# A language model's two blocks on one core: all sixteen tiles of the second mixer turned by token behind the attention units

## What is computed

```
def step(S, inp):
    r_t, w_t, k_t, v_t, a_t, b_t = inp
    Sa = jnp.einsum('bhij,bhj->bhi', S, a_t)
    S = S * w_t[:, :, None, :] + Sa[..., None] * b_t[:, :, None, :] + v_t[..., None] * k_t[:, :, None, :]
    return S, jnp.einsum('bhij,bhj->bhi', S, r_t)
...
o_fox = forgetting_attention(fh(fq), fh(fk), fh(fv), ff, fox_forget_bias[l])
o_rwkv = rwkv7_time_mix(p_rwkv, shift_mu[l], ...)
mix = jnp.concatenate([o_fox, o_rwkv], axis=-1) @ w_out[l]
```

## Time and profile before

| | us |
|---|---|
| median of 3 runs | 3400.59 |
| lowest, highest | 3396.19, 3407.8 |
| the profiled execution | 3394.34 |
| its span | 3392.6 |

### The profile page before, as it was taken

The page is one execution under the profiler, slowest core; times in us unless marked ns, Lnnn a source line. Parts: engine busy times, 40 slices in busy tenths (PEclk is TensorE's granted clock), DMA queues, the critical chain, the costliest instruction groups (busy, mean ns, idle before and its releaser), DMA issues.

```text
span 3392.6 us, 50022 instructions
## 1 busy us (share of the span) xinstructions
PE 3306.0 (97%) x18459; PEld 2704.5 (80%) x18459; DVE 1931.4 (57%) x3749; ACT 1254.7 (37%) x1622; POOL 132.2 (4%) x54
## 2 busy tenths in 40 slices
PE   8998999999899999999999999999999999999998
PEld 6665877878577788888878887888888888888886
DVE  5455456552565544452355999998885444444443
ACT  3333233322455433342343334444544333333332
POOL 0000000000000000000001545000000000000000
PEclk9987999999999999999999999999999999999999
DMA  4110012323222222222332444455556655555542
GB/s 145 56 38 1 4 51 81 99 93 100 86 65 67 80 76 79 80 74 93 100 106 79 148 141 143 156 180 182 185 177 220 228 198 192 198 194 196 198 142 81
DMA packets 145995, 408.03 MB, mean 120 GB/s; under 512 B 11225, under 2 KB 43993, under 8 KB 143585
## 3 DMA queue, kind: packets, MB, share of 16 engines
q1 hardware_dynamic: 73520, 265.85, 25.7%
q10 hardware_dynamic: 72368, 140.68, 11.5%
HBM read 337.28 MB, written 69.21 MB: 120 GB/s over the span
## 4 chain that ended last, share of the span: by engine, by line
PE 87%; DVE 10%; ACT 1%; issue 1%; DMA 1%; ACTq 0%; DVEq 0%; SPq 0%
PE bank L337 24%; PE bank L339 24%; PE bank L338 24%; PE bank L959 2%; PE bank L445 2%; PE bank L957 2%; PE bank L889 1%; ACT arena L1000 1%; PE bank L464 1%; DVE arena L2057 1%; PE bank L503 1%; DVE arena L2020 1%; DVE arena L2021 1%; DVE arena L2023 1%; PE bank L372 1%
## 5 line engine op out<-in xcount | busy, mean ns | idle before, releaser
L337 PE MATMUL bank<-xs,ring_hi 128*128 128x512 f32 x2488 | 990.9, 398 | 19.9 <-DVE xs L1564 9.7
L339 PE MATMUL bank<-xs,ring_lo 128*128 128x512 f32 x2488 | 971.8, 391 | 0.0
L338 PE MATMUL bank<-xs,ring_hi 128*128 128x512 f32 x2488 | 971.3, 390 | 0.0
L1000 ACT ACTIVATE arena<-bank 128x512 f32<-128x512 f32 (+4 forms) x584 | 392.1, 706 | 1013.1 <-PE bank L339 726.8
L1000 ACT ACTIVATE ring_hi<-ring 128x1024 fp32r<-128x1024 f32 x503 | 532.4, 1061 | 621.4 <-DMA ring<-weights 425.3
L1557 DVE TENSOR_TENSOR ring_lo<-ring,ring_hi 128x1024 fp32r<-128x1024 f32 x246 | 300.2, 1224 | 519.5 <-ACT ring_hi L1000 484.0
L337 PEld LDWEIGHTS bank<-xs,ring_hi 128*128 128x128 f32 x2488 | 468.8, 188 | 127.9 <-issue 14.4
L339 PEld LDWEIGHTS bank<-xs,ring_lo 128*128 128x128 f32 x2488 | 468.3, 188 | 100.9
L338 PEld LDWEIGHTS bank<-xs,ring_hi 128*128 128x128 f32 x2488 | 469.2, 189 | 97.1 <-issue 3.4
L2070 DVE TENSOR_TENSOR ring_lo<-ring,ring_hi 128x1024 fp32r<-128x1024 f32 x206 | 252.6, 1226 | 387.3 <-ACT ring_hi L1000 387.2
L337 PE MATMUL bank<-gw,ring_hi 128*128 128x512 f32 x1024 | 398.5, 389 | 0.7 <-ACT arena L1000 0.7
(11 more groups left out here) (285 smaller groups left out, 3408.4 us busy)
## 6 DMA issues: line engine op xcount, KB each, us to landing
ring<-weights SPq DMA_DIRECT2D x503, 512.0 KB, 3.6
hidden<-arena ACTq DMA_DIRECT2D x128, 256.0 KB, 4.1
gates<-arena ACTq DMA_DIRECT2D x16, 2048.0 KB, 6.6
arena<-hidden ACTq DMA_DIRECT2D x16, 2048.0 KB, 10.3
arena<-gates ACTq DMA_DIRECT2D x16, 2048.0 KB, 16.9
xres<-x_t ACTq DMA_DIRECT2D x4, 512.0 KB, 6.5
out_t<-arena SPq DMA_DIRECT2D x4, 512.0 KB, 3.0
arena<-ret_decay ACTq DMA_DIRECT2D x1, 1024.0 KB, 5.9
```

What stands on the lines that cost most here:

```text
L337: pe.matmul(out_, wh, x[0], start=start, stop=False, skip_group_check=True)
L338: pe.matmul(out_, wh, x[1], start=False, stop=False, skip_group_check=True)
L339: return pe.matmul(out_, wl, x[0], start=False, stop=stop, skip_group_check=True)
L1000: return act.activation(out_, in_, f, **kw)
```

## The change

The six tiles leave the units. All sixteen are turned behind the units in one loop, with the same two banks and the same rule (tile j waits for the copy of tile j-2). The order becomes TA, TB, TK, RV, pairs 0 to 3 of each. The semaphores `tok_ready` and `tok_out` are gone, and with them the waits for bank 1 in the units. The count of ACT's copies in `rw_act`, and of PE's tiles in `rw_pe`, goes from 30 to 36 wherever it is waited for. Nothing is added or left out: the same 64 transposes and 16 copies are issued.

```diff
@@ tensor engine, rw_prepare
-                if u in (19, 20, 23, 24, 27, 28):
-                    i, g0 = (u - 19) % 4, (u - 19) // 4
-                    pe.wait_ge(rw_dve, 2 * g0 + 2)
-                    if 2 * g0 + i:
-                        pe.wait_ge(tok_out, 2 * g0 + i)
-                    for g in range(TT):
-                        tr = pe.transpose(bank[1][:, g * P:(g + 1) * P], tile((TA, TB)[i] + g0)[:, g * P:(g + 1) * P], cc("ident"))
-                    tr.then_inc(tok_ready, 1)
                 if u in (17, 21, 25, 29):
                     pe.wait_ge(rw_dve, 2 * m + 1)
-                    if m:
-                        pe.wait_ge(tok_out, 2 * m)
                     pe.matmul(bank[1][:, :], cc("bones"), tile(RKR), start=True, stop=True).then_inc(rw_pe, 1)
@@ tensor engine, behind the units
             pe.wait_ge(rw_dve, 8)
-            pe.wait_ge(tok_out, 2 * (NPAIR - 1))
-            late = [(TA, 3), (TB, 3)] + [(TK, m) for m in range(NPAIR)] + [(RV, m) for m in range(NPAIR)]
-            for j, (src, m) in enumerate(late):
+            for i, (src, _) in enumerate(((TA, MA), (TB, MB), (TK, MK), (RV, MV))):
+                for m in range(NPAIR):
+                    j = 4 * i + m
                     if j >= 2:
                         pe.wait_ge(rw_act, 20 + j - 1)
@@ scalar engine, rw_prepare
-                if u in (20, 21, 24, 25, 28, 29):
-                    i, g0 = (u - 20) % 4, (u - 20) // 4
-                    act.wait_ge(tok_ready, 2 * g0 + i + 1)
-                    A(tile((MA, MB)[i] + g0), bank[1][:, :], ACT.Copy).then_inc(tok_out, 1)
@@ scalar engine, behind the units
-            late = [(MA, 3), (MB, 3)] + [(MK, m) for m in range(NPAIR)] + [(MV, m) for m in range(NPAIR)]
-            for j, (dst, m) in enumerate(late):
-                act.wait_ge(rw_pe, 20 + j + 1)
-                A(tile(dst + m), bank[j % 2][:, :], ACT.Copy).then_inc(rw_act, 1)
+            for i, dst in enumerate((MA, MB, MK, MV)):
+                for m in range(NPAIR):
+                    act.wait_ge(rw_pe, 20 + 4 * i + m + 1)
+                    A(tile(dst + m), bank[(4 * i + m) % 2][:, :], ACT.Copy).then_inc(rw_act, 1)
```

More of the change, by code:

```diff
@@ L221, in build @@
         shifted = sem("shifted")
-        tok_ready, tok_out = sem("rwkv_by_token_psum"), sem("rwkv_by_token")
         ffn_pair, ffn_silu, root_arg = sem("ffn_pair"), sem("ffn_gate_activated"), sem("root_argument")
@@ L572, in _ @@
                     if r == 0:
-                        pe.wait_ge(rw_act, 30)
+                        pe.wait_ge(rw_act, 36)
                     else:
-                        pe.wait_ge(rw_act, 30 + RW_ACT - 1 + s)
+                        pe.wait_ge(rw_act, 36 + RW_ACT - 1 + s)
                         pe.wait_ge(rw_dve, 8 + RW_DVE)
@@ L609, in _ @@
                             keep_clock(7, 1)
-                        pe.wait_ge(rw_act, 30 + RW_ACT * r + 2 * lev + s + 1)
+                        pe.wait_ge(rw_act, 36 + RW_ACT * r + 2 * lev + s + 1)
                         chunks(bank[b0 + 2], tile(hs[b]), tile(hs[4 + a])).then_inc(rw_pe, 1)
@@ L633, in _ @@
                     hs, b0 = HS[s], 3 * s
-                    pe.wait_ge(rw_act, 30 + RW_ACT * r + 10 + 3 * s + 1)
+                    pe.wait_ge(rw_act, 36 + RW_ACT * r + 10 + 3 * s + 1)
                     chunks(bank[b0 + 2], tile(hs[5]), tile(hs[7])).then_inc(rw_pe, 1)
-            base_pe, base_act, base_dve = 30 + RW_PE * 2, 30 + RW_ACT * 2, 8 + RW_DVE * 2
+            base_pe, base_act, base_dve = 36 + RW_PE * 2, 36 + RW_ACT * 2, 8 + RW_DVE * 2
             shv = arena[:, SH:SH + 4, :].rearrange("p a b -> p (a b)").rearrange("p (c n) -> p c n", c=NCH)
@@ L1140, in _ @@
             pair_copy(NPAIR - 1)
-            late = [(MA, 3), (MB, 3)] + [(MK, m) for m in range(NPAIR)] + [(MV, m) for m in range(NPAIR)]
-            for j, (dst, m) in enumerate(late):
-                act.wait_ge(rw_pe, 20 + j + 1)
-                A(tile(dst + m), bank[j % 2][:, :], ACT.Copy).then_inc(rw_act, 1)
+            for i, dst in enumerate((MA, MB, MK, MV)):
+                for m in range(NPAIR):
+                    act.wait_ge(rw_pe, 20 + 4 * i + m + 1)
+                    A(tile(dst + m), bank[(4 * i + m) % 2][:, :], ACT.Copy).then_inc(rw_act, 1)
             for r in range(2):
-                pb = 30 + RW_PE * r
+                pb = 36 + RW_PE * r
                 for lev in range(5):
@@ L1165, in _ @@
                 A(XS[k][0], tile(OF + k), ACT.Copy).then_inc(hi_ready, 1)
-            bp = 30 + RW_PE * 2 + 22
-            ba = 30 + RW_ACT * 2
+            bp = 36 + RW_PE * 2 + 22
+            ba = 36 + RW_ACT * 2
             for m in range(NPAIR):
@@ L1703, in _ @@
             st(TTN(dv(2)[:, :, 0:NCH - 1], dv(1)[:, :, 0:NCH - 1], dv(0)[:, :, 1:NCH], ALU.mult))
-            ve.wait_ge(rw_act, 30)
+            ve.wait_ge(rw_act, 36)
             def mask8(name, half):
@@ L1715, in _ @@
                     if r:
-                        ve.wait_ge(rw_act, 30 + RW_ACT - 1 + s)
+                        ve.wait_ge(rw_act, 36 + RW_ACT - 1 + s)
                     for e in range(2):
@@ L1738, in _ @@
                         TTN(tile(hs[4 + b]), bank[b0 + 2][:, :], tile(hs[4 + a]), ALU.add).then_inc(rw_dve, 1)
-            bp, bd = 30 + RW_PE * 2, 8 + RW_DVE * 2
+            bp, bd = 36 + RW_PE * 2, 8 + RW_DVE * 2
             shv = arena[:, SH:SH + 4, :].rearrange("p a b -> p (a b)").rearrange("p (c n) -> p c n", c=NCH)
@@ L1746, in _ @@
                 if c == 0:
-                    ve.wait_ge(rw_act, 30 + RW_ACT * 2)
+                    ve.wait_ge(rw_act, 36 + RW_ACT * 2)
                     CP(tile(UU + g)[trow, :], tile(U0 + g)[trow, :]).then_inc(rw_dve, 1)
@@ L1773, in _ @@
                 st.go(TSM(tile(RG + m), tile(RG + m), pp("ln_w", m), None, ALU.mult))
-            ba = 30 + RW_ACT * 2 + 4
+            ba = 36 + RW_ACT * 2 + 4
             for m in range(NPAIR):
```

## The result

| | us |
|---|---|
| the kernel before, median of 6 runs (3391.18 to 3410.45) | 3398.39 |
| the changed kernel, median of 6 runs (3370.05 to 3380.3) | 3374.01 |
| ratio, with its 95% interval | 0.9931 (0.9911 to 0.9952) |
| profiled execution and its span | 3374.08, 3372.3 |

The changed kernel is 0.7% faster, 24 us by the medians and 20.3 us by the two profiled executions. The forecast was 3395, with a range down to 3384: the direction was right, the size was not.

A forecast was written before the change was run, and what follows sets the result against it. The prediction took PE, busy for 97% of the span, as the bound. Its terms, +4.0 - 4.4 - 6.6 + 1.0 = -6.0 us with the clock at 0, put the median of 3400.59 at 3395, range 3384 to 3408.

The forecast's parts named there:

- The late loop: Two-bank transpose loop behind the units: six more tiles, three pairs by 1.34 us, wholly on the path, +4.0 us.
- The waits: PE's waits for ACT within the units, 3.4 us before L540 and 3.2 us before L546, go: -6.6 us.
- L540's work: Six groups of transposes leave PE's units; nothing covers them, so all their time goes: -4.4 us.
- Late next: In the units, freed of the stalls, PE will now and then wait for DVE: +1.0 us.
- The clock's term: PE's granted clock in the units goes between two levels; no net direction seen, so left at 0.
- Rival B: In the units the clock stays up where the stall made it fall: 3388, or 3383 with a second stretch; chance 0.22.
- Rival C: In the units the clock's rises are lost with the four transposes ahead of them: +6.4 us, 3407; chance 0.19.
- Rival D: Clock is down in the sixteen tiles behind the units and the products after them: middle +14 us, 3415; chance 0.05.
- Rival E: In the units PE waits for ACT's copies of probabilities instead, so the stalls are replaced: no change, 3400; chance 0.08.

The follow-up runs named there:

- e3: The changed kernel with 24 transposes added on PE within the units, where L540 stood, never copied and without waits for ACT: 3367.72 us, ratio 0.9933.
- e1: The kernel before, its six tiles still turned within the units, but ACT copies each in the unit that turned it, so the waits go: 3368.4 us, ratio 0.9933.
- e2: The changed kernel with the six waits of PE for ACT copies put back, without transposes in the units: 3398.78 us, ratio 1.0019.
- e8: The kernel of e10 with one filler matmul behind each of the four groups of head sums in unit 13: 3369.01 us, ratio 0.9922.
- e10: The kernel of e1 with four banks instead of two in the loop behind the units: 3368.14 us, ratio 0.9933.
- e4: The kernel before, all waits kept, with two filler matmuls on PE ahead of each of the six waits for ACT: 3380.82 us, ratio 0.9964.
- e6: The kernel before with only L540's waits removed, as ACT copies TA one unit earlier and TB as before: 3386.52 us, ratio 0.9969.

## Why the prediction was wrong

*The late loop, +4.0:* right. It took 11.2 us instead of 7.2, at 0.67 us a tile, at clock 1.00.

*The waits, -6.6:* they went as said, all six of them. That part stands.

*L540's work, -4.4:* "Nothing covers them" held only at the clock of before. At full clock DVE bounds the units and covers the 24 transposes: with them (e3, e1) the stretch from unit 21 on took 34.2 and 33.9 us, without them 34.4. So moving the tiles gained nothing by itself and cost the 4.0 us of the loop; what paid was that the waits went.

*Late next, +1.0:* right in kind and size, not in place. PE waited 1.2 us for DVE at L535 (L546 before), in units 25 and 29. In unit 21, where the margin of 0.6 us had been worked out, it did not wait.

*The clock's term, 0:* this step failed. I had both sides of it in view, the stalls at the falls and the transposes at the rises, called the net direction unknown, and put no value to it. The units lost 26.3 us where the sum had 10.0 (4.4 and 6.6 less 1.0); the 16 us between are this term (20 or so if L540's 4.4 us are counted as not gained). The runs decide it. The waits alone take the gain back (e2), and without them the transposes do no harm (e1, e3). Rival B was the right mechanism, with a chance of 0.22 where it should have led. The trace of before held the hint: each of the three falls behind unit 19 came at or behind a stall of 0.95 to 1.5 us, and the full clock from 245.5 on had lasted through units 18 and 19, which have none.

*Rival B's price* was too small as well: 3383 at its far end. It took the two long stretches to full clock, but left the third one (307.45 to 313.75), which held 5.1 us of work at half clock: another 2.4 us. With it B's units are 24.2 us shorter, and they measured 26.3; the 2.1 us between have no cause shown. That B's sum still comes to 20.2 us of the 20.3 between the two profiled executions is luck in part, since the 2.0 us lost outside the units make up for them. From the medians (24.4) the distance is larger, and the scatter of either kernel covers it.

*Rival C, the rises are lost with the transposes:* not in the time. But e2, which has the waits without the transposes, was 0.2% slower than the kernel before, where the sum of its parts (+4.0 for the loop, -4.4 for L540) gives no change. Its clock came up later and less. So the transposes may help a rise; that is argued from one profile and one ratio, not shown.

*Rival D* was the rule of the Trainium skill ("TensorE: Matmul & The Clock Gate", Part 4: PE-mode transpose) that transposes don't count for the clock. Here the clock stayed at 1.00 over the 11.25 us in which PE ran only the 64 of them, and it was still 1.00 in the products behind, so the trace disagrees for these float32 transposes.

*Rival E* did not come: no wait for the probabilities' copies within the units, only the known ones at the very end (2.0 us, before 1.3).

The range ended at 3384 because B's far end was cut off as unlikely; with the leading case right it would have lain below.

## What to carry to other kernels

A stall of PE costs more than its length where it lets the granted clock fall, which here it did at eight of twelve: taking away 6.6 us of waiting and nothing else (e1) gave 0.67% of 3392.6 us, 22.7 us. Where a trace shows the clock go to and fro, look at what stands just ahead of each fall, and price its removal as the work of the following stretch at the other clock, bounded by the next engine. Then price the rest of the change again in that state: work that was on the path before (L540, 4.4 us) may be covered in it. The cure needn't be to move the work: letting ACT copy each tile in the unit in which it was turned (e1) gave the same gain and kept the shorter loop behind.

## What the runs showed of the chip

- One program came back to full clock at very different moments: 247 and 271 us in two executions of the changed kernel, taken at different times, with the same instructions ahead and PE busy throughout (24.00 of 24.00 us from 222 to 246 in the first, at clock 0.51). The two took 3374.08 and 3385.99 us.
- In every profile the clock fell to 0.50 while the 32 matmuls with two columns each ran (L511, in e8 with fillers between them), from 0.2 us behind their start (e10) to 3.5 us (e4). What brings that fall isn't shown.
- Idle time of PE and falls go together without one length that decides: 1.62 us ending at 267.05 in e6 brought none, 0.74 us ending at 249.53 in e4 was followed by one, and the 1.48 us that PE waits for DVE behind the loop brought none in any profile.
- Transposes of float32 on PE kept the clock at 1.00 over 11.25 us, with PE idle for 0.2 us in each 1.34 and for 0.69 us at the end.
